# Summing gathered V rows four tokens at a time instead of two in a hybrid encoder block

## What is computed

```python
q = (hf @ w_q).astype(f32).reshape(t, PEER_HEADS, 2, PEER_HALF)
scores = jnp.einsum('thpd,pkd->thpk', q, sub_keys.astype(f32))
...
idx = (e1 * N_KEYS + e2).reshape(t, PEER_HEADS * PEER_TOPK)
gates = jax.nn.softmax(top_s, axis=-1).reshape(t, PEER_HEADS * PEER_TOPK)

def block(args):
    hb, ib, gb = args
    act = jax.nn.gelu(jnp.einsum('td,tkd->tk', hb, u_tab[ib]).astype(f32), approximate=False)
    return jnp.einsum('tk,tkd->td', (gb * act).astype(hb.dtype), v_tab[ib])
```

## Time and profile before

| | us |
|---|---|
| median of 3 runs | 3441.29 |
| lowest and highest run | 3439.2 and 3469.48 |
| the profiled execution's own time | 3440.77 |
| its span, first to last instruction | 3438.6 |
| TensorE busy | 2559.1 |
| VectorE busy | 2035.7 |
| POOL busy | 1961.4 |
| ScalarE busy | 539.0 |

### The profile page before, as it was taken

One profiled execution on the slowest core, in us unless ns is written; L12 is line 12 of the kernel. 1 busy time (PEld: TensorE's weight loads), 2 busy tenths in 40 slices (PEclk: granted clock), 3 DMA queues, 4 the chain that ended last, 5 costly groups with the idle time before them and its releaser, 6 DMA issues.

```text
span 3438.6 us, 27456 instructions
## 1 busy us (share of the span) xinstructions
PE 2559.1 (74%) x9080; PEld 1052.6 (31%) x9080; DVE 2035.7 (59%) x4748; ACT 539.0 (16%) x1185; POOL 1961.4 (57%) x2094
## 2 busy tenths in 40 slices
PE   8995879677885787677885776577875677656787
PEld 6863554133322333234321322123212312111111
DVE  4438787466676656765576656765667556655300
ACT  3433542022121122111110001000000001000000
POOL 1003343666656666665656666666666666666665
PEclk9997999899998998899987887897987899777799
DMA  7416886999999999999999998999999999999998
GB/s 242 161 41 251 292 315 248 387 390 372 386 350 384 373 370 369 368 384 342 379 344 396 375 355 341 383 384 354 369 366 402 344 370 367 375 368 374 370 373 327
DMA packets 355213, 1181.05 MB, mean 343 GB/s; under 512 B 41968, under 2 KB 72304, under 8 KB 354816
## 3 DMA queue, kind: packets, MB, share of 16 engines
q0 software_dynamic: 296368, 1078.14, 82.2%
q1 hardware_dynamic: 57552, 96.97, 8.1%
q10 hardware_dynamic: 1152, 4.19, 0.3%
HBM read 1157.20 MB, written 21.42 MB: 343 GB/s over the span
## 4 chain that ended last, share of the span: by engine, by line
POOL 35%; PE 22%; issue 15%; DMA 10%; another core or an unknown queue 8%; DVE 4%; ACT 2%; SPq 0%; ACTq 0%; DVEq 0%; POOLq 0%
POOL ring L932 35%; PE y_psum L1014 6%; DMA ring<-in_peer_v_dram,picks_T 6%; PE tile_psum L1167 4%; PE b_bank L968 3%; DMA ring<-in_peer_u_dram,picks 3%; DVE ring L1399 2%; PE y_psum L968 2%; PE tile_psum L1146 2%; PE tile_psum L1110 1%; PE tile_psum L1109 1%; PE tile_psum L1091 1%; DMA res<-in_w_units_dram 1%; DMA ring<-in_w_units_dram 0%
## 5 line engine op out<-in xcount | busy, mean ns | idle before, releaser
L1399 DVE CUSTOM_DVE_ANT_0 ring<-ring,h_psum 128x1024 f32<-128x1024 f32 x1024 | 1232.7, 1218 | 737.6 <-DMA ring<-in_peer_u_dram,picks 637.6
L1014 PE MATMUL y_psum<-ring,spread 128*32 128x512 f32 x4096 | 1345.2, 669 | 404.5 <-DMA ring<-in_peer_v_dram,picks_T 328.2
L932 POOL DMA_INDIRECT ring<-in_peer_u_dram,picks x1024 | 969.9, 947 | 737.3 <-issue 286.1
L932 POOL DMA_INDIRECT ring<-in_peer_v_dram,picks_T x1024 | 967.5, 945 | 613.0 <-issue 274.1
L1014 PEld LDWEIGHTS y_psum<-ring,spread 128*32 128x32 f32 x4096 | 267.3, 116 | 1366.3 <-DMA ring<-in_peer_v_dram,picks_T 735.9
L1167 PE MATMUL tile_psum<-w_q,arena 128*128 128x512 f32 x512 | 250.1, 638 | 54.9 <-issue 53.4
L968 PE MATMUL b_bank<-ring 128*128 128x384 f32 (+1 forms) x544 | 200.6, 512 | 9.1 <-issue 7.7
L1167 PEld LDWEIGHTS tile_psum<-w_q,arena 128*128 128x128 f32 x512 | 102.7, 203 | 200.0 <-issue 195.0
L1257 ACT COPY spread<-zero 128x8 f32<-128x8 f32 (+1 forms) x104 | 21.6, 208 | 724.7 <-remote 434.7
L968 PEld LDWEIGHTS b_bank<-ring 128*128 128x128 f32 (+1 forms) x544 | 101.1, 193 | 104.7 <-issue 57.5
L1429 DVE SCALAR_TENSOR_TENSOR res<-res,stat_e,final_row 128x1024 f32<-128x1024 f32 x8 | 10.2, 1272 | 185.1 <-ACT stat_e L1274 185.1
(11 more groups left out here) (245 smaller groups left out, 2336.6 us busy)
## 6 DMA issues: line engine op xcount, KB each, us to landing
ring<-in_w_units_dram SPq DMA_DIRECT2D x42, 512.0 KB
ring<-in_peer_u_dram,picks POOLq DMA_INDIRECT x1024
ring<-in_peer_v_dram,picks_T POOLq DMA_INDIRECT x1024
arena<-in_w_units_dram SPq DMA_DIRECT2D x28, 512.0 KB, 3.8
ring<-in_w_q_T_dram SPq DMA_DIRECT2D x16, 512.0 KB, 3.6
res<-in_w_units_dram SPq DMA_DIRECT2D x14, 512.0 KB
arena<-tok_scr SPq DMA_DIRECT2D x7, 768.0 KB
w_q<-in_x_dram SPq DMA_DIRECT2D x8, 512.0 KB, 9.7
```

The source lines that it names most:

```text
L932: pool.indirect_dma_start(ring[:, j], None, tables[kind], bass.IndirectOffsetOnAxis(ap=at, axis=0)).then_inc(filled[j], 16)
L1014: last = nc.tensor.matmul(y_ps[quad * STEPS:(quad + 1) * STEPS, half], lines[:, quad, at:at + STEPS], ring[:, j, half * BANK:(half + 1) * ...
L1399: nc.vector.tensor_tensor_reduce(out=ring[:, j], in0=ring[:, j], in1=h_ps[:], scale=1.0, scalar=0.0, op0=ALU.mult, op1=ALU.add, accum_out= ...
```

## The change

V items now stand in runs of four in the list, and TensorE sums the four tokens of a run in one call at the last of them: left half of tokens A, B, C, D, then right half of A, B, C, D, each in its own column quarter. The shares of V items are rounded to fours instead of twos. No gather, matmul or copy is added or removed, and each token goes to the same quarter as before.

```diff
 def with_spreads(v, age):
-    return [("V", v, age), ("V", v + 1, age)] + [("E", b, age) for b in range(2, N_SPREADS) if v + 2 == last_token(b - 2) + 5]
+    return [("V", v + n, age) for n in range(QUADS)] + [("E", b, age) for b in range(2, N_SPREADS) if v + QUADS == last_token(b - 2) + 5]
...
-    v_marks = tuple((at, begun + before * part // 20 * 2) for at, part in v_shares)
+    v_marks = tuple((at, begun + before * part // (10 * QUADS) * QUADS) for at, part in v_shares)
...
-    for u_end, v_end in zip(share_ends(u_marks), share_ends(v_marks, 2)):
+    for u_end, v_end in zip(share_ends(u_marks), share_ends(v_marks, QUADS)):
...
-            pick(u0 + (u_end - u0) * (v + 2 - v0) // (v_end - v0 + 1))
+            pick(u0 + (u_end - u0) * (v + QUADS - v0) // (v_end - v0 + 1))
             seq += with_spreads(v, 1)
-            v += 2
+            v += QUADS
...
-        while v < ahead * n // (2 * left) * 2:
+        while v < ahead * n // (QUADS * left) * QUADS:
             seq += with_spreads(v, 0)
-            v += 2
+            v += QUADS
...
-                if kind == "V" and n % 2:
-                    pair(n - 1, back, e)
+                if kind == "V" and n % QUADS == QUADS - 1:
+                    sum_step(n // QUADS, back, e)
...
-            def pair(v, back, e):
-                step = v // QUADS
+            def sum_step(step, back, e):
                 b, at = SPREAD_OF[step]
                 at *= STEPS
-                if at == 0 and v % QUADS == 0:
+                if at == 0:
                     pe.wait_ge(s["spread_ready"], N_SPREADS * (e - back) + b + 1)
                 lines = spread[SPREADS[b][0]]
-                tokens = [("V", v + n, back) for n in range(2)]
+                tokens = [("V", step * QUADS + quad, back) for quad in range(QUADS)]
```

## The result

The changed kernel takes **3517.38 us** (median of 4 runs, 3508.57 to 3530.11) against 3445.81 us for the kernel before on the same chip: ratio 1.0198, 95% interval 1.0139 to 1.0257. Three later comparisons, on three different chips, gave 1.0179 [1.0125, 1.0232], 1.0145 [1.0111, 1.0179] and 1.0197 [1.0167, 1.0226]. So the change costs 53 to 72 us. The forecast was 3447 us, no change that can be told, with a range up to 3488: the median lies 29 us above the range.

The account below looks back on a forecast made before the run. The prediction took the DMA engines as the bound, with no more than 90 us of their idle time to be had. 3440.8 + 18 - 17 + 5 = 3446.8, median 0.5 us above: 3447 us, range 3403 to 3488.

Parts of the forecast that it names:

- The first step, ready sums: TensorE's V sums: 57 blocks fewer at 1.9 us, at most 108 us, counting only where TensorE is late.
- The second step, the hold: Ring of 8, stages 1 to 3: first slots held over three more landings instead of one; +18 us.
- The margin of 1.1 us: Ring of 8: how late TensorE may be before POOL feels it, after the change; 4.2 us before.
- the bound above: Stages 1 to 3: most added POOL waiting from held slots, 23 runs waiting 3.1 us longer, 71 us.
- The third step, relief: Where TensorE is late, POOL's second wait falls away: a third of 104.0 us, half let through, -17 us.
- The fourth step, the order: V items in fours, U gathers in runs of three to six: +5 us, bounds nothing and 21 us.
- 12 slots "should not notice": Stages 4 to 8: margin still 6.5 us after the change; lengths to stay within 1%.
- The end: After the last landing: the same two steps release the last sums, so no move.
- The clock: TensorE's granted clock stays within 0.05; a 0.05 fall in stages 1 to 6 would show 8 us. No separate chance.
- the ring of 8 chokes: Rival, stages 1 to 3: most runs cost POOL 1 to 3 us more; about 3490 to 3510 us; chance 0.22.
- decision point: Stages 1 to 3: the slower rival decides once POOL's wait for TensorE exceeds 104 + 79 us.
- other sign: Stages 1 to 3: DMA share at 0.93 or less, with "remote" gone, would show the slower rival.

Follow-up runs that it names:

- the order alone: Changed kernel with TensorE summing in pairs again, list and shares still in fours; 1.0068 and, on another chip, 1.0054 of the kernel before.
- the late release alone: List in fours with pair sums, plus POOL waiting for a run's fourth token before reusing its first or second token's slot; 1.0491 of the kernel before.

## Why the prediction was wrong

**What bounds the kernel** was read rightly: DMA idle time caused by late slots is what a change can touch, and TensorE's busy time is not. TensorE lost 157 us of it and nothing was gained.

**The first step, ready sums,** held. The group of V sums fell by 196 us where 100 or more was expected, off the path. The Trainium skill (TensorEngine Tiling (Array Packing), Theoretical Speedup) has up to 4 for tiles of 32; here the group went from 1345.2 to 1149.3 us, a factor of 1.17, since pairs were wide already and the rest is waiting for rows.

**The second step, the hold, is the one that failed**, in the size of its term. The margin of 1.1 us was worked out rightly, but 36 us of added waiting were taken, the middle between nothing and 71, and the relief was set against them with 35. So POOL's wait for TensorE was to stay where it was. It grew by 97 us in the first pair of profiles, and by 70 between the two kernels that differ in the sums alone: the bound above, with nothing to set against it. Not 23 waits grew by 3.1 us each, but nearly all by 0.9. Their number hardly moved (56 to 63; 94 to 81 on a faster chip) and their mean went from 2.1 to 2.9 us (1.6 to 2.6 there). That the bound came out right is luck in that sense. Then half was let through for the cover by "remote", with no look at how much cover there was. The cover was real but finite: between those two kernels it took 47 us and was gone. +18 should have been +27 to +35 in stages 1 to 3, and +46 to +56 on a chip without it. The mean spacing of 1.53 us hid that too: where landings come at 1.24 us, as in a burst of ready slots, the margin is by the same estimate below zero.

**The third step, relief,** -17 us, did not come from the sums of four. What there is of it comes from the order alone, which took 15.7 us (11.3 on a faster chip) off POOL's wait for TensorE, where 35 were expected, and it was more than eaten up by the wait for VectorE. The sums of four took 14 us (19 to 23 on faster chips) off the wait for VectorE, which no term had.

**The fourth step, the order,** +5 us, measured 21 (3478.32 - 3457.41; 3269.01 - 3248.27): its upper bound, and not in the places named. On one chip 11 of it lie in stage 0, for which the prediction had no term; on the other 5.5 in stage 0 and 15.1 in stages 1 to 3 (1127.1 against 1112.0 with the kernel before's order). The wait that it lengthened there was POOL's for VectorE, by 22.8 us; that fits the longer runs of U gathers, of which the prediction said that they do not pile up by themselves, but was not tried apart. With +27 or more for the hold, nothing for the relief, 21 for the order and 11 in stages 4 to 6, the sum would have come near the 53 to 72 us that were measured.

**12 slots "should not notice"** held on two faster chips to 2 us of 1016, as long as the run of four stands together. On a slower chip they grew by 3 us with the list and 11 more with the sums, and in the first pair of profiles by 21.5 us or 1.9%, past the 1% foreseen. What does that was not found. The profiles scatter here: five of the same program in these stages on slower chips have 1134.5 to 1142.4 us, two of the kernel before 1119.4 and 1128.5.

**The end** did not move: stage 8 took 200.3 us against 201.2, stage 7 301.1 against 299.8.

**The clock** fell by more than the 0.05 allowed in stages 4 and 6 (0.85 to 0.79, 0.88 to 0.81). But it was 0.82 with the order alone, where the three stages took 1131.6 us against 1128.5 before, so the fall went with some 3 us; it was not tried by itself. The Trainium skill (TensorE: Matmul & The Clock Gate, Loop structure matters more than you think) says that a long wait for DMA between matmuls makes them slow. The traces neither confirm nor refute it: the clock fell from 0.86 to 0.82 while the waiting for V rows went only from 325.9 to 342.8 us (order alone), and from 0.82 to 0.81 while it went to 457.3.

**The rival that came true** is "the ring of 8 chokes", given 0.22. Its decision point, a wait for TensorE beyond 104 + 79 = 183 us, was passed in all four profiles of the changed kernel (201.1, 191.1, 185.3, 195.0), and "remote" went as it said. Its other sign, a DMA share of 0.93 or less, did not: the share was 0.95. Its times, 3490 to 3510, lie 7 us and more under the median, and rest on a slip: 106 runs at 1 us with no cover are 106 us and not 53, which with the +5 of the order would be some 3550 us. That its times lie so near is partly luck.

**Open:** the 8 to 16 us of stage 0, which on the two faster chips need both the list in fours and the four-wide sums (374 to 382 us with one of them, 388 to 389 with both) and on a slower one only the list (386.6 with pair sums); the part of stages 4 to 6; the excess of the late release alone; and why both halves of a token at once, with its early release, did not bring the time back.

## What to carry to other kernels

Batching the consumer of a ring lengthens the hold of its first slots by the landings of the others. Work out the round trip against slots times spacing, and where the margin left is less than one landing, expect nearly every wait of today to grow and take the upper bound for the sum, not the middle. The producer's idle waits covered the added wait here up to about their sum in those stages: compare the two, rather than halve. The reverse did not hold: in one run the idle waits came back and the time did not. A coarser order of a shared list moves waits as well, here from TensorE to VectorE. Before counting on a wider operation, see whether neighbours already overlap, and whether the engine's time ends anything.

## What the runs showed of the hardware

The kernel before took 3446 to 3457 us in four comparisons and 3245 and 3248 us in the two on two other chips. In stage 8, V gathers alone, POOL issues one each 1.24 us, and on those two chips the DMA takes them at that pace (393 to 407 GB/s up to the last gathers, 409 in stage 7; stage 8 in 182 to 186 us with 12 slots or pairs; no wait in "remote"). On the others it is 364 to 373 GB/s, stage 8 takes 198 to 201 us in the kernels before and changed, and POOL is in "remote" for 27 to 52 us of it. That the same late slot costs more on the faster chips fits POOL being the limit there; no run tried it by itself. A ratio is only to be read within one chip.

Sixteen instructions of two separate calls, for four column quarters, take the time of eight. So the order of a list alone, which put such calls next to each other, took 146 us off the busy time of the V sums, and the wider call only 46 more.
